# Gate products of three merges cut into pieces and moved, with one weight split moved ahead of a mix

## What is computed

```python
def _merge(ym, ya, yh, gpre, mb, wm, wa, wh, wo):
    g = jax.nn.sigmoid((gpre + mb).astype(jnp.float32)).astype(ym.dtype)
    g_m, g_a, g_h = jnp.split(g, 3, axis=-1)
    y = g_m * (ym @ wm) + g_a * (ya @ wa) + g_h * (yh @ wh)
    return y @ wo
```

## Time and profile before

| | before |
|---|---|
| median of 3 runs | 2970.01 us (2967.67 to 2970.2) |
| the profiled execution, its own time | 2966.67 us |
| its span in the trace | 2964.5 us |
| TensorE busy | 2659.3 us (90% of the span) |
| VectorE busy | 1439.9 us (49%) |
| ScalarE busy | 938.6 us (32%) |
| mean bandwidth | 208 GB/s |
| granted TensorE clock, mean | 0.969 of full |

### The profile page before, as it was taken

One profiled execution on the slowest core, in us unless ns is written; L12 is line 12 of the kernel. 1 busy time (PEld: TensorE's weight loads), 2 busy tenths in 40 slices (PEclk: granted clock), 3 DMA queues, 4 the chain that ended last, 5 costly groups with the idle time before them and its releaser, 6 DMA issues. The chain is left out here.

```text
span 2964.5 us, 40742 instructions
## 1 busy us (share of the span) xinstructions
PE 2659.3 (90%) x15853; PEld 1947.3 (66%) x15853; DVE 1439.9 (49%) x2691; ACT 938.6 (32%) x1615; POOL 0.2 (0%) x4
## 2 busy tenths in 40 slices
PE   6998999989999897999988889899899987988887
PEld 3886866657787775555544659877689885544444
DVE  6676745567455676211112577455555555222222
ACT  5222255542333322111101253445545452110000
POOL 0000000000000000000000000000000000000000
PEclk9999999989999998999999989999999998999999
DMA  6333511033211442799999423321233146999998
GB/s 278 136 142 145 185 64 64 29 139 143 81 58 57 158 183 95 320 426 429 429 424 427 174 80 114 132 86 57 78 114 107 65 153 253 429 428 428 428 426 350
DMA packets 58233, 615.98 MB, mean 208 GB/s; under 512 B 7726, under 2 KB 9712, under 8 KB 11120
## 3 DMA queue, kind: packets, MB, share of 16 engines
q1 hardware_dynamic: 57584, 613.91, 51.7%
q10 hardware_dynamic: 512, 0.25, 0.0%
HBM read 613.08 MB, written 1.05 MB: 207 GB/s over the span
## 5 line engine op out<-in xcount | busy, mean ns | idle before, releaser
L191 PE MATMUL ps<-rounded,rounded 128*128 128x256 f32 (+1 forms) x1856 | 634.4, 342 | 48.7 <-DVE rounded L182 26.1
L192 PE MATMUL ps<-rounded,rounded 128*128 128x256 f32 (+1 forms) x1856 | 624.4, 336 | 0.0
L193 PE MATMUL ps<-rounded,rounded 128*128 128x256 f32 (+1 forms) x1856 | 624.1, 336 | 0.0
L182 DVE TENSOR_TENSOR rounded<-low_arena,rounded 128x1024 fp32r<-128x1024 f32 (+2 forms) x348 | 371.6, 1091 | 246.5 <-ACT rounded L178 242.4
L191 PEld LDWEIGHTS ps<-rounded,rounded 128*128 128x128 f32 x1856 | 356.9, 192 | 92.7 <-issue 23.7
L193 PEld LDWEIGHTS ps<-rounded,rounded 128*128 128x128 f32 x1856 | 356.8, 192 | 35.6
L192 PEld LDWEIGHTS ps<-rounded,rounded 128*128 128x128 f32 x1856 | 357.2, 192 | 34.8 <-issue 0.5
L178 ACT ACTIVATE rounded<-low_arena 128x1024 fp32r<-128x1024 f32 (+3 forms) x344 | 313.6, 950 | 185.5 <-PE ps L193 110.9
L167 PE MATMUL ps<-high_arena 128*128 128x256 f32 (+3 forms) x1072 | 262.2, 397 | 36.1 <-DVE high_arena L655 12.9
L2328 PE MATMUL ps<-high_arena,low_arena 128*64 128x256 f32 x2240 | 254.5, 385 | 26.7 <-DMA high_arena<-in_e_w 15.0
L2785 PE MATMUL ps<-high_arena,low_arena 128*64 128x256 f32 x2048 | 235.9, 386 | 42.8 <-DMA high_arena<-in_e_w 30.7
(11 more groups left out here) (470 smaller groups left out, 2913.6 us busy)
## 6 DMA issues: line engine op xcount, KB each, us to landing
high_arena<-in_e_w SPq DMA_DIRECT2D x191, 2048.0 KB, 20.2
low_arena<-in_d_wm SPq DMA_DIRECT2D x48, 1024.0 KB, 4.8
low_arena<-in_d_wml SPq DMA_DIRECT2D x32, 1024.0 KB, 4.8
low_arena<-in_d_wh SPq DMA_DIRECT2D x16, 1536.0 KB, 6.3
high_arena<-in_d_modlater SPq DMA_DIRECT2D x24, 1024.0 KB, 4.9
low_arena<-in_d_wa SPq DMA_DIRECT2D x16, 1536.0 KB, 6.2
low_arena<-in_d_modlater SPq DMA_DIRECT2D x16, 1024.0 KB, 6.4
low_arena<-in_d_wo SPq DMA_DIRECT2D x8, 1024.0 KB, 4.9
```

The costliest lines, as they stand in the source:

```text
L182: return v.tensor_tensor(lo, raw, hi.bitcast(F32), ALU.subtract)
L191: pe.matmul(out, l_hi, r_hi, start=(k == 0), stop=False)
L192: pe.matmul(out, l_lo, r_hi, start=False, stop=False)
L193: last = pe.matmul(out, l_hi, r_lo, start=False, stop=(k == n - 1))
```

## The change

Five edits. In the hyena the gates of unit 0 are cut into chunks 0 to 5, at the old place, and chunks 6 and 7 behind `turn(7)`; the gates of unit 1 into chunks 0 to 3, at the old place, and 4 to 7 behind the last `synthesise`. VectorE's split of the first gate weights moves from behind head 6's `mix` to ahead of it. In attention and mLSTM only chunks 0 to 3 of gate 1 stay at the end of the stage; chunks 4 to 7 move behind the barrier, to the head of TensorE's list in the merge, ahead of unit 0. No instruction is added or removed, and no transfer is moved.

```diff
+GATE_SPLIT = 4
@@ stage_hyena, TensorE
             pe.wait_ge(convolved, (KC - 2) * 3 + 1)
-            gate_products(pe, K, l, 2, ahead, 0, range(KC))
+            gate_products(pe, K, l, 2, ahead, 0, range(6))
             synthesise(KC - 2)
             turn(KC - 1, 1)
+            gate_products(pe, K, l, 2, ahead, 0, range(6, KC))
             analyse(KC - 1)
             pe.wait_ge(convolved, KC * 3)
-            gate_products(pe, K, l, 2, ahead, 1, range(KC))
+            gate_products(pe, K, l, 2, ahead, 1, range(4))
             synthesise(KC - 1)
+            gate_products(pe, K, l, 2, ahead, 1, range(4, KC))
@@ stage_hyena, VectorE, step(u, s)
+                if not weights:
+                    split_ahead(v, K, 2, ahead, 0)
                 mix(ch, u, s)
                 if weights:
                     weight(u + 2, s, 2)
-                else:
-                    split_ahead(v, K, 2, ahead, 0)
@@ stage_merge, TensorE
+            if branch != 2:
+                gate_products(pe, K, l, branch, ahead, 1, range(GATE_SPLIT, KC))
             pe.wait_ge(ahead.done, 2)
             pe.sem_inc(projected, 1)
             unit(0, 0, gated_ahead=True)
@@ stage_attention, TensorE
             pe.wait_ge(v_copied, KC)
-            gate_products(pe, K, l, 1, ahead, 1, range(KC))
+            gate_products(pe, K, l, 1, ahead, 1, range(GATE_SPLIT))
@@ stage_mlstm, TensorE
             pe.wait_ge(unit_out, 2 * LAST)
-            gate_products(pe, K, l, 0, ahead, 1, range(KC))
+            gate_products(pe, K, l, 0, ahead, 1, range(GATE_SPLIT))
```

## The result

The changed kernel took 2950.35 us (median of 4 runs, 2946.43 to 2950.95); the kernel before took 2970.11 us beside it (4 runs, 2967.67 to 2972.68). The ratio is 0.9929, with a 95% interval of 0.9915 to 0.9943: 21 us faster by the ratio, 19.8 by the medians. A second set of 6 runs gave 2949.47 and 0.9932 (0.9921 to 0.9944). The forecast was 2953.8, with 2946 to 2960 as its range.

What follows compares the result with a forecast made beforehand. TensorE, busy 90% of the span, bounds the kernel, so only idle and low-clock time can be won. Terms 4.5 + 0.2 + 4.4 + 4.6 + 0.8 + 1.7 = 16.2 us off 2966.67 give 2950.5, plus 3.3 for the median: 2953.8, range 2946 to 2960.

Steps and rivals of the forecast that it cites:

- Hyena, layer 0: Hyena's end and the merge behind it, layer 0: S 7.0 us earlier, less 2.5 us of low clock, net 4.5 us won.
- S: Start of ScalarE's first rounding in a merge; forecast at 271.1 instead of 278.15 behind the hyena of layer 0.
- the rival's case: Low clock also behind the 2.1 us wait inside the hyena, layer 0, costing 2 us; part of a rival with chance 0.18.
- Attention's merge, layer 0: Attention's end and merge, layer 0: twelve gates leave the block, 2.7 us, less 2.5 us of low clock: 0.2 us won.
- mLSTM's merge, layer 0: mLSTM's end and merge, layer 0: 2.7 us from twelve gates plus 1.7 us from a vanished low-clock stretch: 4.4 us won.
- Hyena, layer 1: Hyena and its merge, layer 1: unit 2 comes 5.8 us earlier, less 1.2 us booked for low clock: 4.6 us won.
- Attention's merge, layer 1: Attention's merge, layer 1: S gains 1.35 us, ScalarE's tile wait 0.9, a new 3 us wait costs 1.5: 0.8 us won.
- mLSTM's merge, layer 1: mLSTM's merge, layer 1: twelve gates leave the block, 1.35 us at full and 2.5 at low clock; 1.7 us won.
- The clock holds: Rival: full clock across the new waits of 3 to 4.3 us, so 23.9 us won, 2946.1 us; chance 0.15.
- It falls more often: Rival: low clock also in layer 0's hyena, mLSTM's merge and both small layer 1 merges; 11.7 us won, 2958.3; chance 0.18.
- The ends did move: Denies the rival that another engine releases the barriers, so stage ends stay: 0 to 2 us lost, 2970 to 2972; chance 0.04.
- the clock stays down: Rival: once down behind the long waits of three openings, the clock stays low, 25 us each giving 2983.6 us; chance 0.03.

## Why the prediction was right

The total was 3.5 us too high. The mechanisms held at nearly every place, but part of the agreement of the terms is luck of the clock, named below. Its terms against the one profiled execution, each measured from a milestone ahead of its place, so that what happened earlier drops out:

**Hyena, layer 0: 4.5 forecast, 4.3 measured.** From head 6's forward transform (240.53, after: 240.72) unit 2 came after 54.30 us and now after 48.39, 5.9 sooner. The clock of 0.73 over 5.9 us behind it costs 0.27 x 5.9 = 1.6. The forecast had 7.0 and 2.5. The first gates came at 245.68 for 245.2, the first transform at 249.86 for 249.2, S at 272.60 for 271.1. Two steps were mis-sized, and together they let the last inverse transform begin at 265.95 for 264.4. The first is the end of the modulations. The forecast let the last two begin up to 0.5 us earlier than at 256.15; their tile came later instead, and the second gate split began at 260.17 for 259.4, with VectorE's next mix behind it:

```profile
256.36 1.23 DVE L970 SCALAR_TENSOR_TENSOR low_arena<-low_arena 128x1024 f32<-128x1024 f32 x1 [2.52 <-DMA low_arena<-in_d_modlater]
...
260.17 1.22 DVE L182 TENSOR_TENSOR rounded<-low_arena,rounded 128x1024 fp32r<-128x1024 f32 x1
...
264.43 0.69 DVE L954 TENSOR_TENSOR high_arena<-high_arena 128x512 f32<-128x512 f32 x1
```

The second is the twelve gates of unit 1, booked at 2.7 us beside a mix that hides them: behind their wait of 2.13 us the clock was 0.62, they took 4.57 us, and the transform began 0.8 us behind the mix's end (265.12). That the clock falls at this place was the rival's case, and it is no luck: it fell here in all nine traces that have this wait.

**Attention's merge, layer 0: 0.2 forecast, 1.2 measured.** From the last sums to unit 2 it takes 21.88 us for 24.76, 2.9 sooner, forecast as 2.7, with a wait of 3.09 us forecast as 3.8. The clock (0.69 over 5.5 us) takes 1.7, forecast as 2.5. The twelve gates behind the barrier delayed unit 0 a little: it begins 3.46 us behind S for 3.06, and the wait ahead of unit 2 absorbs that.

**mLSTM's merge, layer 0: 4.4 forecast, 4.5 to 6.0 measured.** From the transposes to unit 2 it takes 22.12 us for 26.46. 1.5 of these 4.3 us are luck: before, the gates behind the wait of 2.36 us ran at 0.67 (24 in 7.31 us), here at 1.00 (12 in 3.00); in the second execution they ran at 0.64, and the way took 23.66, 2.8 sooner for a forecast of 2.7. The low stretch of 1.7 us behind the old wait of 2.82 is gone in both, as forecast; but in the kernel with the hyena's edits alone, where that wait is still 2.76 us, it is gone too (1.00 over 6.1 us), so the traces don't show that the shorter wait removed it.

**Hyena, layer 1: 4.6 forecast, 6.1 measured.** Unit 2 was 12.95 us early where the layer begins (1756.44 to 1743.49 is its start) and was 13.0 + 6.1 = 19.0 early at its end (1883.62 to 1864.62). The gross had been put at 5.8; the 1.2 us for a low clock behind unit 2 weren't due, since the wait is 1.23 us and not 2.4. Nearly half of the 6.1 is luck of the clock in the execution of before. In the kernel with the pieces across the barriers alone the hyena is unchanged, and there the same wait ahead of the first gates (3.71 us) was followed by 1.00 over 5.6 us for 0.52 before; the way to unit 2 took 29.91 us for 32.84, and 26.79 in the changed kernel. The edits themselves win 3.1 us of it, the rest is the low clock behind a wait that they shorten to 1.59 us.

**Attention's merge, layer 1: 0.8 forecast, a loss of 1.9 and a gain of 2.5 measured.** Here the executions differ. From the last sums to unit 2 it took 16.40 us before, 15.64 and 13.95 after, for a forecast of 2.3 sooner. ScalarE's second pair of roundings shows why, first in the changed kernel, then in its second execution:

```profile
2115.79 2.00 ACT L178 ACTIVATE rounded<-low_arena 128x1024 fp32r<-128x1024 f32 x2 [2.32 <-DMA low_arena<-in_d_wm]
```

```profile
2120.50 2.01 ACT L178 ACTIVATE rounded<-low_arena 128x1024 fp32r<-128x1024 f32 x2 [0.88 <-DMA low_arena<-in_d_wm]
```

S was at 2107.22 and 2113.37, so ScalarE got the tile 8.57 and 7.13 us behind S. What is late next is the tile of unit 2, as the forecast allowed when it took 0.9 of 2.15 us, and it doesn't land after the same time twice, though it is issued 2.35 us behind S in both. Nor did S gain the 1.35 us of the forecast: it begins 2.94 and 2.70 us behind the start of the last sums for 3.88, since VectorE ends there as late as TensorE. Behind the long wait the clock was 0.56 over 6.1 us, a loss of 2.7; behind 1.94 us it was 1.00.

**mLSTM's merge, layer 1: 1.7 forecast, 0.6 and 1.6 measured** from the transposes to unit 2 (17.39 us before, 16.79 and 15.78 after). In the first the gates on both sides of the barrier ran at 0.58 (2366.66 to 2372.25).

The measured terms sum to 4.3 + 1.2 + 6.0 + 6.1 - 1.9 + 0.6 = 16.3 us for the span's 16.5 in this execution. That they sum so well is partly chance: the three of layer 0 give 11.5 us where layer 1 begins 12.95 early, and the last two lose 1.3 where the span loses 2.5. Stretches between them also changed clock: attention's gates in layer 0 ran at 0.50 before and 1.00 after (12 in 5.49 and 3.02 us), others the other way round.

**The rivals.** *The clock holds* came true in neither execution of the changed kernel at unit 2 of the first two merges, but it did hold behind 3.06, 3.39 and 3.71 us in three places of the experiments, so the rival was a fair one. *It falls more often* came true at the first of its four places, not in mLSTM's merge of layer 0, and in layer 1 once in each: at unit 2 of attention's merge in the first execution (3.38 us, 0.56), at unit 2 of mLSTM's in the second (1.77 us, 0.68). The ends did move. That the clock stays down didn't happen: behind the new waits all low stretches are over within some 6 us. The rule that the Trainium skill's page "TensorE: Matmul & The Clock Gate" gives in "HAM oscillation", that the clock drops at each long wait, is what the runs show in the mixers and their merges behind 3.8 us and more; between 1.6 and 3.7 us they show both. The same page's remark in "What's actually happening", that one kernel finds the activity watch in different phases, is what two executions show at 1.59 and 2.36 us; it makes a sum by single low stretches good to some 2 us a place, and no better.

## What to carry to other kernels

Look first for a single instruction that another engine waits for and that stands behind work wanted only later: one VectorE instruction moved ahead of a mix brought as much as all the hyena's edits together. At a barrier look at which engine ends second, not only last: moving half of the gates of unit 1 behind it let unit 2 come 2.9 us sooner in attention of layer 0, moving the other half too let ScalarE begin only 0.35 sooner, since VectorE came only that much ahead of TensorE. Gates put into a wait are worth its length only if the wait doesn't come back further on, where it may also lower the clock. When a chain holds the next unit a fixed time behind the barrier, look into the chain: of two transfers of 1024 KB each, issuing the one that is awaited first ahead of the other, and without a wait that it didn't need, took away a wait of 3.4 us there and won some 6 us in all, with no instruction added.

## What the runs showed of the hardware

- **Equal waits, unequal clocks.** Behind a wait of 1.59 us the granted clock was 0.50, 1.00 and 0.50 in three executions of before, after and after again, behind one of 2.36 us 0.67, 1.00 and 0.64, behind 2.04 us (layer 1) 0.66, 0.58 and 0.69. Behind 3.38, 3.39, 3.31 and 3.43 us ahead of the same unit 2 (layer 1, attention's merge, four kernels) it was 0.56, 1.00, 0.55 and 0.57. Behind waits of 3.72 and 3.71 us ahead of the hyena's first gates in layer 1 (before, and the pieces across the barriers alone) it was 0.52 and 1.00. Behind unit 2's waits of 0.81 to 1.39 us it was 1.00 in every trace, but a short wait is no warrant elsewhere: behind 0.93 us at 363.5 in attention of the changed kernel it was 0.66 over 5 us.
- **One place, one clock.** Behind the wait ahead of unit 1's gates in the hyena of layer 0, 2.01 to 2.44 us long, it was 0.62 over 4.5 us in eight traces and 0.64 in the ninth. In the kernel with only the split moved the wait there was 1.03 us and the clock 1.00.
- **The first matmul behind a barrier.** TensorE began its products 0.45 us behind its last ones ahead of the barrier when it was itself the last to come (layer 0, attention and mLSTM), and 0.47 us behind VectorE's end when VectorE was (986.90 to 987.37).
- **A transfer's landing moves by 1.4 us** between two executions of one kernel that issue it at the same time behind S (2.35 us; the tile is there 8.57 and 7.13 us behind S), which is as much as a whole term of the forecast.
